# Expert rows of U and V gathered by two DMAs from two arrays, instead of one DMA from a joined array

## The reference

```python
def chunk(args):
    hx, idx, g = args          # 128 tokens: activations, expert numbers [128, 128], gates [128, 128]
    a = jax.nn.gelu(jnp.einsum("ced,cd->ce", u_emb[idx], hx), approximate=False)
    return jnp.einsum("ce,ced->cd", g * a, v_emb[idx])
```

## Time and profile before

| | |
|---|---|
| median of 3 executions | 1879.97 us (1879.29 to 1881.41) |
| profiled execution | 1877.61 us, span 1875.80 us |
| PE busy | 1578.3 us, 84% of the span |
| DVE busy | 954.3 us, 51% |
| ACT busy | 546.8 us, 29% |
| POOL busy | 302.9 us, 16% |
| DMA queue of POOL's transfers | 279.20 MB, 38.4% of the 16 DMA engines' span |
| the experts' stage | from 420.6 us (first gather) to 1090.4 us (last slot on PE), 36% of the span |

### The profile page before, as it was taken

One profiled execution on the slowest core, in us unless ns is written; L12 is line 12 of the kernel. 1 busy time (PEld: TensorE's weight loads), 2 busy tenths in 40 slices (PEclk: granted clock), 3 DMA queues, 4 the chain that ended last, 5 costly groups with the idle time before them and its releaser, 6 DMA issues.

```text
span 1875.8 us, 18232 instructions
## 1 busy us (share of the span) xinstructions
PE 1578.3 (84%) x7014; PEld 1111.6 (59%) x7014; DVE 954.3 (51%) x1788; ACT 546.8 (29%) x1170; POOL 302.9 (16%) x296
## 2 busy tenths in 40 slices
PE   7999799897777777777777769888899979979998
PEld 5777578484222222222222249654899869649996
DVE  1994431235676766767674443322555444235554
ACT  1002430013323232332323233332333334323333
POOL 2000000003433444444344300120000000000000
PEclk9999559998999999999999989699899979589999
DMA  9963003339999999999999914032344434034551
GB/s 247 206 199 135 1 1 135 135 128 384 419 417 420 420 420 420 418 402 420 420 418 420 413 50 166 23 118 90 135 180 182 182 123 160 17 135 163 189 187 45
DMA packets 52022, 428.68 MB, mean 229 GB/s; under 512 B 6880, under 2 KB 7032, under 8 KB 9824
## 3 DMA queue, kind: packets, MB, share of 16 engines
q0 software_dynamic: 40720, 279.20, 38.4%
q1 hardware_dynamic: 11216, 148.33, 20.9%
HBM read 422.50 MB, written 4.98 MB: 228 GB/s over the span
## 4 chain that ended last, share of the span: by engine, by line
PE 62%; DMA 22%; DVE 9%; ACT 4%; issue 2%; POOL 0%; DVEq 0%; SPq 0%; ACTq 0%; POOLq 0%
PE psum L585 23%; DMA pool<-uv,experts 21%; PE psum L676 9%; PE psum L677 9%; PE psum L678 9%; PE psum L791 6%; PE psum L634 3%; DVE pool L1431 3%; PE psum L618 3%; DMA ring<-stream 1%; DVE w_lo L1215 1%; ACT diag L1062 1%; ACT xn L880 1%; DVE hT L1150 1%; ACT coef L1056 1%
## 5 line engine op out<-in xcount | busy, mean ns | idle before, releaser
L791 PE MATMUL psum<-pool,diag 128*128 128x512 f32 x1024 | 487.5, 622 | 167.4 <-ACT diag L1062 167.1
L791 PEld LDWEIGHTS psum<-pool,diag 128*128 128x128 f32 x1024 | 191.0, 196 | 463.3 <-ACT diag L1062 253.3
L1431 DVE CUSTOM_DVE_ANT_0 pool<-pool,xn 128x1024 f32<-128x1024 f32 x256 | 313.7, 1227 | 213.6 <-DMA pool<-uv,experts 208.6
L542 POOL DMA_INDIRECT pool<-uv,experts x256 | 270.9, 1058 | 765.0 <-DVE experts L1408 385.9
L1215 DVE TENSOR_TENSOR w_lo<-ring,w_hi 128x2048 fp32r<-128x2048 f32 x86 | 196.8, 2292 | 219.3 <-ACT w_hi L937 219.3
L937 ACT ACTIVATE w_hi<-ring 128x2048 fp32r<-128x2048 f32 x86 | 164.0, 1911 | 325.8 <-PE psum L678 325.8
L676 PE MATMUL psum<-h_hi,w_hi 128*128 128x256 f32 x704 | 200.8, 285 | 22.4 <-DVE h_lo L1226 22.4
L677 PE MATMUL psum<-h_lo,w_hi 128*128 128x256 f32 x704 | 200.5, 285 | 0.0
L678 PE MATMUL psum<-h_hi,w_lo 128*128 128x256 f32 x704 | 200.4, 285 | 0.0
L585 PE MATMUL psum<-hT,ring 128*128 128x256 f32 x768 | 170.3, 385 | 5.1 <-DMA ring<-stream 2.5
L585 PEld LDWEIGHTS psum<-hT,ring 128*128 128x128 f32 x768 | 147.9, 193 | 26.7 <-issue 3.2
(11 more groups left out here) (208 smaller groups left out, 1918.1 us busy)
## 6 DMA issues: line engine op xcount, KB each, us to landing
ring<-stream SPq DMA_DIRECT2D x66, 2048.0 KB, 7.6
pool<-uv,experts POOLq DMA_INDIRECT x256, 12.7
ring<-stream SPq DMA_DIRECT2D x3, 1024.0 KB, 4.9
t_scratch<-att POOLq DMA_DIRECT2D x1, 2048.0 KB, 93.8
rpb_scratch<-att POOLq DMA_DIRECT2D x7, 256.0 KB, 29.3
ring<-stream SPq DMA_DIRECT2D x1, 1792.0 KB, 8.8
row<-rows POOLq DMA_DIRECT2D x1, 1672.0 KB, 15.3
ring<-stream SPq DMA_DIRECT2D x1, 1664.0 KB, 6.9
```

The costliest lines, as they stand in the source:

```text
L542: gp.indirect_dma_start(out=gath[:, n % NROWS, :], out_offset=None, in_=uv, in_offset=bass.IndirectOffsetOnAxis(ap=experts[:, n:n + 1], ax ...
L791: last = nc.tensor.matmul(sums[half], diag[:, n % NDIAG, :], gath[:, n % NROWS, D + 512 * half:D + 512 * half + 512], start=k == 0, stop=k ...
L1431: ins = V.tensor_tensor_reduce(out=row_u, in0=row_u, in1=xn[:, n // SLOTS, :], scale=1.0, scalar=0.0, op0=ALU.mult, op1=ALU.add, accum_out ...
```

## The change

Each slot gets two gathers of 128 rows of 4 KB, one from `u_rows` into `ugath` and one from `v_rows` into `vgath`. Both have eight buffers, and together they take the same memory as `gath`. A U buffer is free when its pair's dots are done, a V buffer when PE has finished its slot. DVE waits for the U row alone, and PE has a wait of its own for the V row. The bytes are the same.

```diff
-        gath = view(pool, 0, NROWS, 2 * D)
+        ugath = view(pool, 0, NROWS, D)
+        vgath = view(pool, NROWS * D, NROWS, D)
...
                 if n >= NROWS:
+                    gp.wait_ge(dots_ready, (n - NROWS) // 2 + 1)
+                gp.indirect_dma_start(out=ugath[:, n % NROWS, :], out_offset=None, in_=u_rows,
+                                      in_offset=bass.IndirectOffsetOnAxis(ap=experts[:, n:n + 1], axis=0)
+                                      ).then_inc(u_landed_in[n % NROWS], 16)
+                if n >= NROWS:
                     wait_spent(gp, n - NROWS)
-                gp.indirect_dma_start(out=gath[:, n % NROWS, :], out_offset=None, in_=uv,
+                gp.indirect_dma_start(out=vgath[:, n % NROWS, :], out_offset=None, in_=v_rows,
                                       in_offset=bass.IndirectOffsetOnAxis(ap=experts[:, n:n + 1], axis=0)
-                                      ).then_inc(row_landed_in[n % NROWS], 16)
+                                      ).then_inc(v_landed_in[n % NROWS], 16)
...
                     pe.wait_ge(diag_ready, n + 1)
+                    pe.wait_ge(v_landed_in[n % NROWS], 16 * (n // NROWS + 1))
                     for half in range(2):
                         last = nc.tensor.matmul(sums[half], diag[:, n % NDIAG, :],
-                                                gath[:, n % NROWS, D + 512 * half:D + 512 * half + 512],
+                                                vgath[:, n % NROWS, 512 * half:512 * half + 512],
...
-                dve.wait_ge(row_landed_in[n % NROWS], 16 * (n // NROWS + 1))
-                row_u = gath[:, n % NROWS, 0:D]
+                dve.wait_ge(u_landed_in[n % NROWS], 16 * (n // NROWS + 1))
+                row_u = ugath[:, n % NROWS, :]
```

More of the change, by code:

```diff
@@ L204, in __init__, with build @@
         self.scale, self.table, self.sinks, self.column = scale, table, sinks, column
-def build(nc, stream, consts, t5const, params, rows, keys_in, late_rows, x_in, positions, t5_in, rpb_in, uv, out):
+def build(nc, stream, consts, t5const, params, rows, keys_in, late_rows, x_in, positions, t5_in, rpb_in, u_rows, v_rows, out):
     with ExitStack() as ctx:
@@ L396, in build @@
         gates_ready = sem("gates_ready")
-        row_landed_in = [sem("row_landed_in%d" % b) for b in range(NROWS)]
+        u_landed_in = [sem("u_landed_in%d" % b) for b in range(NROWS)]
+        v_landed_in = [sem("v_landed_in%d" % b) for b in range(NROWS)]
         row_spent = sem("row_spent")
@@ L1643 @@
     late = np.concatenate([a["final_gain_2"], a["od_v_gain_2"][0]])[None]
-    uv = np.concatenate([a["peer_u"][0], a["peer_v"][0]], 1)
     consts, t5 = shape_constants()
@@ L1648 @@
         "x_in": a["x"].reshape(S, D), "positions": a["positions"].reshape(NT, P).T, "t5_in": a["t5_bias_2"],
-        "rpb_in": a["od_rpb_2"][0], "uv": uv, "keys_in": keys,
+        "rpb_in": a["od_rpb_2"][0], "u_rows": a["peer_u"][0], "v_rows": a["peer_v"][0], "keys_in": keys,
     }
```

## The result

The changed kernel takes 1952.75 us (median of 4, 1950.42 to 1955.82) beside 1880.69 us for the kernel before (median of 4): ratio 1.038, 95% interval 1.0365 to 1.0404. The forecast was 1964 us, with a range of 1890 to 2005.

A forecast was written before the change was run, and what follows sets the result against it. The prediction took the DMA queue as the bound before and POOL after: 636.2 us of issues, 1.3 plain DMA, 3.5 selection and 102.4 dot holds, less 9.0 at the tail, put the stage 84.3 us later: 1964 us, 80% range 1890 to 2005.

The forecast's parts named there:

- The bound: Gather stage: the full DMA queue sets the pace before, at 2.549 us a slot; POOL's issues and holds after, about 2.9.
- The issue's price: POOL: a gather costs 0.94 us plus 0.30 to the next, whatever its bytes; 511 intervals of 1.245 us are 636.2 us.
- The holds: POOL gathers starting during a DVE instruction with two SBUF operands stand until it ends: 102.4 us for dots, 3.5 for selection.
- The waits: POOL's waits for free U and V buffers are always met: a 17 us loop against 23 us for eight slots.
- The tail: From the last gather's start to PE's end: 10.7 us instead of 19.7, 9.0 us less.
- The sum: Whole stage: last gather starts 93.3 us later; less 9.0 for the end, the stage ends 84.3 us later.
- The DMA floor: Transfers of 4 KB rows take 2.53 to 2.62 us a slot, which matters only if nothing else is slower.
- What the profile would show: Stage's profile after: DMA share 0.87, rate 360 GB/s, median landing 6 us, gathers' median 0.94 and mean about 1.14 us.
- A: Rival: DMA transfers stay the stage's bound and little happens, 1875 to 1898 us; chance 0.15.
- B: Rival: faster, 1866 to 1874 us, if a pair of POOL issues costs less than a slot's 2.549 us; chance 0.06.
- C: Rival: POOL's gathers and DVE's dots lock each other out fully, 3.7 us a slot, about 2170 us; chance 0.01.
- D: Rival: late landings or a slow PE make POOL wait for buffers again, 2040 us and more; chance 0.08.

The follow-up runs named there:

- experiment 3: Kernel before with a second gather of 64 bytes a row after each gather, its 8 KB rows kept: 1948.05 us, ratio 1.0392.
- experiment 5: Changed kernel with the U buffer freed by PE's slot, as the V buffer is, instead of by the dots: 1949.34 us, ratio 1.0367.
- experiment 6: Changed kernel with V's gather fetching only the first 2 KB of each row from the ninth slot on: 1977.29 us, ratio 1.052.
- experiment 1: Changed kernel with the dot reading its second operand, the activation, from PSUM instead of SBUF: 1895.37 us, ratio 1.0098.
- experiment 4: Kernel before with a second gather of 64 bytes a row after each gather, and the dots' activation in PSUM: 1899.32 us, ratio 1.0118.
- experiment 8: Changed kernel without the selection of units 1 to 7, all units using unit 0's experts and gates: 1892.16 us, ratio 1.0076.
- experiment 2: Kernel before with the dots' activation moved to PSUM: 1881.26 us, ratio 1.0013.

## Why the prediction was right, step by step

- **The bound.** POOL takes the place of the DMA queue: shown by POOL's waits after, and by experiments 3, 5 and 6, which exclude small rows, release and bytes. It does so by issues and holds together (2.49 and 0.36 us a slot); the issues alone would not (experiments 1 and 4).
- **The issue's price.** Forecast 1.245 us whatever the row's size, measured 0.94 + 0.30 for rows of 64 bytes, 4 KB and 8 KB. Without the holds (92.9), the waits (6.6) and the plain DMA (1.3) the 737.0 us between the first and the last start are 636.2 for 511 intervals, as forecast.
- **The holds.** Forecast 105.9 us (0.40 us a dot and 3.5 for the selection); measured (1111 - 941) + (1134 - 941) = 363 ns a slot, 92.9 us. This is the term that was mis-sized, by 13 us. The chance of a hold was put at 0.84 and is 203 of 256, 0.79; its mean was put at 0.525 us and is 0.455. The working took dots to meet gathers at random. They don't: 48 gathers of the changed kernel started with 0.2 to 0.3 us of a dot left and 35 with 1.1 to 1.2, but only 4 to 12 in each tenth from 0.5 to 1.1. Experiments 6 and 8 say the same: 0.106, 0.363 and 0.435 us a slot came out of the same number of dots and gathers. So it is in part luck that 0.40 was near. No long gather had started inside a selection instruction, so the 3.5 us put down for these were not seen. The last unit of the changed kernel, at 1080 to 1157 us, already runs with little hold: 59.01 us of POOL for 60 gathers.
- **That the second SBUF operand is the cause** is shown by experiments 1, 2 and 4: moving one operand took 91 us off the changed kernel's gathers. The rule of the Trainium skill (SBUF — State Buffer, Who interferes with whom) that such an instruction contends with a GpSimd instruction that reads SBUF agrees with the trace, since a gather reads its 128 indices from SBUF. The page's inference on descriptor generation is not refuted by that. The plain DMA of POOL, which reads no indices, was not held by a dot in any of five runs (0.97 us as always; lines below). That the reading of the indices is what waits fits both, but no run takes it away by itself. What doesn't follow from the page is the step that the prediction set against its sum, that by this inference the term would be nothing for gathers.
- **The waits.** Forecast as always met; POOL waited some 7 us beyond the usual gap (2.2 us once for dots; 16.1 us for PE, of which 38 x 0.30 is gap), nearly all of it before the two gathers of the ninth slot, the first that need a used buffer.
- **The tail.** Forecast 10.7 us, measured 11.4.
- **The sum.** +84.3 forecast, +77.1 measured on the profiled executions: 13 too much for holds and 1.35 for the start of the stage, against 7 too little for waits and 0.7 for the tail. So the errors cancel in part. The median is off by 11 and not by 7, because the profiled execution lies 2.0 us above it, where the forecast took 2.4 below.
- **The DMA floor.** 4 KB rows were put at 2.53 to 2.62 us a slot. Experiment 1 shows 1.049 MB at 409 GB/s, 2.56 us, where 8 KB rows have 2.50 to 2.52.
- **What the profile would show.** The rate fell to 366 GB/s (forecast 360), the landing to 6.4 us (6). The DMA share was forecast at 0.87 and stayed at 0.97, as each packet took 6% longer than with a full queue (worked out below): this reading failed.
- **The rivals.** A falls by POOL's waits and by experiment 3. B needed quicker issues, and no gather took under 934 ns. C needed dots that are held: the longest took 1296 ns (1294 before). D needed long waits of POOL, and they come to some 7 us.

## What to carry to other kernels

Splitting a transfer costs nothing only while the engine that issues it has time for twice the issues. Before doubling them, divide the stage by their number and set it beside the time from one start to the next of two issues that wait for nothing. Here that alone, 2.49 against 2.55 us a slot, would have promised no loss. So look at the mean against the median of the issuing instruction, too: what lies between is hidden time that turns into real time when the engine becomes the bound. An operand moved to PSUM bought back 56 of 72 us here, and a buffer freed earlier was worth nothing behind a queue that issues in order.

## What the runs showed of the hardware

- A gather that starts inside a dot with two SBUF operands ends 0.81 us after that dot (means of 0.81 to 0.82 in nine runs, for starts with 0.15 us or more of the dot left). POOL's plain DMA isn't held: in five runs it started with 0.31 to 0.58 us of a dot left and took 0.966 to 0.973 us. Here is one of each, from experiment 3; the dots have 0.54 and 0.53 us left:

```profile
492.70 1.23 DVE L1435 CUSTOM_DVE_ANT_0 pool<-pool,xn 128x1024 f32<-128x1024 f32 x1 [1.68 <-DMA tiny<-tiny_rows,experts]
493.39 1.35 POOL L546 DMA_INDIRECT tiny<-tiny_rows,experts  x1 [0.30 <-issue]
...
514.69 1.22 DVE L1435 CUSTOM_DVE_ANT_0 pool<-pool,xn 128x1024 f32<-128x1024 f32 x1 [1.41 <-DMA tiny<-tiny_rows,experts]
515.38 0.97 POOL L552 DMA_DIRECT2D tab<-t_scratch  x1
```

- The share of DMA time is no gauge of a full queue. From 600 to 1000 us the changed kernel moved 366 GB/s at a share of 0.97, and the version with PSUM 409 GB/s at 1.03. POOL's queue in both, changed kernel first, where packets, MB and share are shown:

```profile
q0 software_dynamic: 40177, 146.29, 97.1%
```

```profile
q0 software_dynamic: 44892, 163.46, 102.4%
```

  That is 0.155 us a packet against 0.146, tiny ones counted in: packets took 6% longer when fewer were waiting. Here the rate tells how full the queue is, when it is set beside the best rate of the same rows (409 GB/s). The median landing (6.4 us against 13.1) tells only whether gathers wait behind each other: experiment 8 had 408 GB/s with landings after 7 us. Why the packets take longer wasn't tried.
- A kernel with holds on its path can vary more from execution to execution. Experiment 3 took 1932 to 1957 us in four, where 13 of the kernel before on the same chip took 1873 to 1882. That the holds differ between these four is likely, but only one of them was traced.
- TensorE's granted clock in the stage's mean fell from 0.97 to 0.92 of its full 2.4 GHz, with PE waiting longer between pairs of slots. It cost nothing that can be seen: PE was busy for 540.7 of the stage's 748.4 us.
